# Hybrid decoder trunk on one core: the rows of the first two experts picked one expert at a time

## What is computed

```
x = x + mixed @ w_out[l]
x = x + hier_moe(rmsnorm(x, norm2_g[l]), router..., moe_w_gate[l], moe_w_up[l], moe_w_down[l])

# hier_moe: the best of 4 groups, the best 2 of its 8 experts; then for each expert, on its own tokens
hdn = jax.nn.silu(xb @ w_gate[e]) * (xb @ w_up[e])
y = hdn @ w_down[e]
# and out[token] += y * weight for the token's two experts
```

## Time and profile before

| | us |
|---|---|
| median of 3 runs | 1980.73 (1980.21 to 1994.71) |
| the profiled execution's own time | 1980.56 |
| its span, first to last instruction | 1978.7 |
| PE busy | 1656.9 (84%) |
| DVE busy | 609.6 (31%) |
| ACT busy | 277.4 (14%) |
| POOL busy | 163.5 (8%) |
| mean granted clock of TensorE | 0.959 of full |

### The profile page before, as it was taken

One profiled execution on the slowest core, in us unless ns is written; L12 is line 12 of the kernel. 1 busy time (PEld: TensorE's weight loads), 2 busy tenths in 40 slices (PEclk: granted clock), 3 DMA queues, 4 the chain that ended last, 5 costly groups with the idle time before them and its releaser, 6 DMA issues. The chain is left out here.

```text
span 1978.7 us, 23018 instructions
## 1 busy us (share of the span) xinstructions
PE 1656.9 (84%) x9408; PEld 979.9 (50%) x9408; DVE 609.6 (31%) x1296; ACT 277.4 (14%) x607; POOL 163.5 (8%) x185
## 2 busy tenths in 40 slices
PE   6999988897998768977489998898889877689772
PEld 3445656556554435544244465664565534345441
DVE  2263265713111123111224523565231111231113
ACT  2212233311000000000113123332100000000001
POOL 0010000002111010101100101000021101101001
PEclk9999999998999999999789999999989999999996
DMA  8312001056899998999651120103568999989995
GB/s 292 101 46 91 1 8 44 6 239 254 353 425 425 426 425 362 424 426 424 274 194 43 50 87 0 52 1 122 207 269 355 426 423 425 425 373 426 426 425 204
DMA packets 72615, 493.51 MB, mean 249 GB/s; under 512 B 24963, under 2 KB 26563, under 8 KB 36704
## 3 DMA queue, kind: packets, MB, share of 16 engines
q1 hardware_dynamic: 60160, 467.76, 57.7%
q0 software_dynamic: 12384, 24.80, 3.3%
HBM read 480.63 MB, written 28.11 MB: 257 GB/s over the span
## 5 line engine op out<-in xcount | busy, mean ns | idle before, releaser
L812 PE MATMUL banks<-RING,XS 128*64 128x256 f32 x3904 | 449.8, 386 | 84.0 <-DMA RING<-in_w_up 49.8
L812 PEld LDWEIGHTS banks<-RING,XS 128*64 128x64 f32 x3904 | 293.9, 139 | 258.4 <-DMA RING<-in_w_up 65.2
L827 PE MATMUL banks<-RING,XS 128*64 128x512 f32 x992 | 226.5, 597 | 39.9 <-DVE XS L1478 21.7
L536 PE MATMUL banks<-RING,XNT 128*128 128x512 f32 x512 | 224.0, 595 | 0.0
L1475 DVE SCALAR_TENSOR_TENSOR XS<-banks,TABLE,XS 128x256 f32<-128x256 f32 x60 | 29.0, 484 | 467.4 <-PE banks L812 467.4
L536 PEld LDWEIGHTS banks<-RING,XNT 128*128 128x128 f32 x512 | 96.6, 191 | 117.3 <-issue 116.8
L827 PEld LDWEIGHTS banks<-RING,XS 128*64 128x64 f32 x992 | 73.8, 136 | 149.8 <-issue 140.7
L1085 ACT ACTIVATE XS<-banks,TABLE 128x256 f32<-128x256 f32 x60 | 28.5, 474 | 827.3 <-PE banks L812 827.3
L1638 POOL DMA_INDIRECT y_rows<-XS,SOLVE x64 | 72.1, 1127 | 659.5 <-DVE XS L1500 659.5
L527 PE MATMUL banks<-XNT,RING 128*128 128x512 f32 x256 | 110.4, 593 | 1.8 <-DMA RING<-in_w_in_blocks 1.8
L1500 DVE COPY XS<-banks 128x512 f32<-128x512 f32 x64 | 44.3, 692 | 216.5 <-PE banks L827 216.5
(11 more groups left out here) (310 smaller groups left out, 1732.6 us busy)
## 6 DMA issues: line engine op xcount, KB each, us to landing
RING<-in_w_up SPq DMA_DIRECT2D x62, 2048.0 KB, 10.1
RING<-in_w_down SPq DMA_DIRECT2D x62, 2048.0 KB, 25.6
RING<-in_w_gate SPq DMA_DIRECT2D x60, 2048.0 KB, 26.5
RING<-in_w_in_blocks SPq DMA_DIRECT2D x12, 2048.0 KB, 8.3
RING<-in_w_out_blocks SPq DMA_DIRECT2D x4, 2048.0 KB, 7.8
TOK<-in_w_gate SPq DMA_DIRECT2D x4, 2048.0 KB, 26.1
y_rows<-TOK SPq DMA_DIRECT2D x4, 1024.0 KB, 25.1
SCAN<-in_w_gate SPq DMA_DIRECT2D x2, 2048.0 KB, 17.9
```

Of the source, the lines that this page charges most:

```text
L536: last = mm(bank[:, :], XNT[:, k, i * P:(i + 1) * P], w[:, k, :], start=(k == 0), stop=(k == KD - 1))
L812: last = mm(bank[f * CAP:(f + 1) * CAP, 0:256], rows[:, k, :], w[:, k, f * 256:(f + 1) * 256], start=(k == 0), stop=(k == KD - 1))
L827: last = mm(PS[5][n * CAP:(n + 1) * CAP, :], HT[:, j, f * CAP:(f + 1) * CAP], w[:, k, n * BN:(n + 1) * BN], start=(k == 0), stop=(k == KF ...
```

## The change

`pick_rows` takes one expert at a time: HOT's 64 columns of that expert are the stationary operand and X is the moving one, in two halves of 512 channels that lie on the two halves of the array, 8 products into bank 6. ACT copies the bank to `FIRST` (64 slots on each half of the partitions), `turn_picked` turns it by 16 products of 64x64 into bank 0 or 1, and DVE copies it with the scale into the expert's half of XT. Expert 1's picks stand behind expert 0's up products, its turning behind the turn of expert 0's hidden rows. DVE's copy for expert 0 stands ahead of the last steps on the slot numbers. And the eight loads of the combine count on two semaphores instead of four, so that the first two tiles wait for four loads together, and the last two for the next four. The diff, cut to its core:

```diff
+FIRST = view(XSb, 3328, BN)
...
-def pick_rows():
+def pick_rows(e):
+    for i in range(NT):
+        for n in range(2):
+            last = mm(PS[6][n * CAP:(n + 1) * CAP, :], HOT[:, i, e * CAP:(e + 1) * CAP], X3[:, i, n * BN:(n + 1) * BN],
+                      start=(i == 0), stop=(i == NT - 1))
+    last.then_inc(picked, 1)
+def turn_picked(e):
+    pe.wait_ge(pick_copied, e + 1)
+    halves = FIRST.rearrange("r (p k) -> r p k", k=KD)
     for k in range(KD):
-        for i in range(NT):
-            last = mm(PS[k // 4][:, (k % 4) * P:(k % 4 + 1) * P], X3[:, i, :].rearrange("t (p k) -> t p k", k=KD)[:, :, k],
-                      HOT[:, i, :], start=(i == 0), stop=(i == NT - 1))
-        if k % 4 == 3:
-            last.then_inc(picked, 1)
+        for n in range(2):
+            part = slice(n * CAP, (n + 1) * CAP)
+            last = mm(PS[e][part, k * CAP:(k + 1) * CAP], halves[part, :, k], ident[part, part], start=True, stop=True)
+    last.then_inc(picked, 1)
...
+    early = e if isinstance(e, int) else NE
+    if h == 0 or early == 1:
+        pe.wait_ge(xt_copied, i + 2 if early else 1)
     gate_or_up(of(0), PS[2], XT[:, :, h * CAP:(h + 1) * CAP]).then_inc(gate_ps, 1)
     gate_or_up(of(1), PS[3], XT[:, :, h * CAP:(h + 1) * CAP]).then_inc(up_ps, 1)
     if h == 1 and not last:
         pe.wait_ge(rows_full, 8 * (NE - 2) * layer + 16 * (i + 1))
         pe.sem_inc(pe_passed, 1)
         turn_rows(P, xt_ps)
+    if early == 0:
+        pick_rows(1)
     pe.wait_ge(hidden, e + 1)
     turn_hidden(ht_ps)
+    if early == 0:
+        turn_picked(1)
     pe.wait_ge(y2_copied, e + 1)
     pe.wait_ge(ht_copied, e + 1)
     down(of(2)).then_inc(y2_ps, 1)
 pe.wait_ge(first_hot, 1)
-pick_rows()
+pick_rows(0)
+turn_picked(0)
...
+def copy_picked(e):
+    act.wait_ge(picked, 2 * e + 1)
+    ac(FIRST, PS[6][:, :], ACT.Copy).then_inc(pick_copied, 1)
+copy_picked(0)
 def gates(first, last):
     for e in range(first, last):
         if e == 2:
             act.wait_ge(table_in, 32 * (layer + 1))
         act.wait_ge(gate_ps, e + 1)
         ac(HS, PS[2][:, 0:256], ACT.Silu, scale=BLK[:, e, 1:2] if e >= 2 else 1.0).then_inc(gated, 1)
+        if e == 0:
+            copy_picked(1)
...
 V.scalar_tensor_tensor(AT[:, :], SPOT, float(NBLK), rv(144, 8), ALU.mult, ALU.subtract).then_inc(routed, 1)
+def copy_picked(e):
+    dve.wait_ge(picked, 2 * e + 2)
+    V.tensor_tensor(XT[:, :, e * CAP:(e + 1) * CAP], PS[e][:, :].rearrange("p (k s) -> p k s", k=KD),
+                    G2K[:, :, None].to_broadcast([P, KD, CAP]), ALU.mult).then_inc(xt_copied, 1)
+copy_picked(0)
 spot_ij = SPOT.rearrange("p (j i) -> p i j", j=2)
 link(V.scalar_tensor_tensor(WTK.rearrange("p (i j) -> p i j", j=2), spot_ij, NE * CAP - 0.5, W2, ALU.is_lt, ALU.mult))
 link(V.tensor_scalar(SPOT, SPOT, -float(NE * CAP), None, ALU.add))
...
-def copy_rows(k0, k1, n):
-    k = k1 - k0
-    return V.tensor_tensor(XT[:, k0:k1, 0:n], PSALL[:, k0 * P:k1 * P].rearrange("p (k s) -> p k s", k=k)[:, :, 0:n],
-                           G2K[:, k0:k1, None].to_broadcast([P, k, n]), ALU.mult)
...
-dve.wait_ge(picked, 1)
-copy_rows(0, 4, P)
-dve.wait_ge(picked, 2)
-copy_rows(4, 8, P).then_inc(xt_copied, 1)
...
     hide(hidden, BLK[:, e, 1:2] if e >= 2 else None)
     dve.wait_ge(ht_ps, e + 1)
     copy_hidden(ht_copied)
+    if e == 0:
+        copy_picked(1)
     if h == 1 and e < NE - 1:
         dve.wait_ge(xt_ps, i + 1)
-        copy_rows(0, 8, P).then_inc(xt_copied, 1)
+        copy_rows().then_inc(xt_copied, 1)
...
-    dve.wait_ge(gathered[i], 32 * (layer + 1))
+    dve.wait_ge(gathered[i // 2], 64 * (layer + 1))
...
-    pool.dma_start(YG[n], yd[j * SEQ + i * P:j * SEQ + (i + 1) * P, :]).then_inc(gathered[i], 16)
+    pool.dma_start(YG[n], yd[j * SEQ + i * P:j * SEQ + (i + 1) * P, :]).then_inc(gathered[i // 2], 16)
```

More of the change, by code:

```diff
@@ L233, in build @@
             ctx.enter_context(nc.semaphore(n)) for n in ("scattered", "table_in", "rows_full"))
-        gathered = [ctx.enter_context(nc.semaphore(f"gathered{i}")) for i in range(NT)]
+        gathered = [ctx.enter_context(nc.semaphore(f"gathered{i}")) for i in range(2)]
         with nc.Block() as block:
@@ L314, in build @@
         combined = sem("combined")
-        first_hot, picked = sem("first_hot"), sem("picked")
+        first_hot, picked, pick_copied = sem("first_hot"), sem("picked"), sem("pick_copied")
         lam_rt, sgu_done = sem("lam_rt"), sem("sgu_done")
@@ L849, in expert @@
                         e = 2 * i + h
-                        if h == 0:
-                            pe.wait_ge(xt_copied, i + 1)
+                        early = e if isinstance(e, int) else NE
+                        if h == 0 or early == 1:
+                            pe.wait_ge(xt_copied, i + 2 if early else 1)
                         gate_or_up(of(0), PS[2], XT[:, :, h * CAP:(h + 1) * CAP]).then_inc(gate_ps, 1)
@@ L1452, in _, with copy_rows @@
                     V.scalar_tensor_tensor(AT[:, :], SPOT, float(NBLK), rv(144, 8), ALU.mult, ALU.subtract).then_inc(routed, 1)
+                    def copy_rows():
+                        return V.tensor_tensor(XT, PSALL[:, 0:2 * BN].rearrange("p (k s) -> p k s", k=KD), G2K[:, :, None].to_broadcast([P, KD, P]),
+                                               ALU.mult)
+                    def copy_picked(e):
[3 more added lines that the diff above has]
+                    copy_picked(0)
                     spot_ij = SPOT.rearrange("p (j i) -> p i j", j=2)
@@ L1455, in _ @@
                     link(V.tensor_scalar(SPOT, SPOT, -float(NE * CAP), None, ALU.add))
-                    cmp = XSb[:, 2048:2048 + NOV * NE].rearrange("p (b e) -> p b e", b=NOV)
+                    cmp = XSb[:, 2304:2304 + NOV * NE].rearrange("p (b e) -> p b e", b=NOV)
                     link(V.tensor_tensor(cmp, ends[:, None, :].to_broadcast([P, NOV, NE]),
```

## The result

The changed kernel takes **1998.8 us** (median of 20 runs, 1987.38 to 2017.25) beside 1986.26 us for the kernel before (median of 20 runs, 1980.21 to 1997.09). The ratio is 1.0072, 95% interval 1.0051 to 1.0092: about 14.3 us slower, between 10.1 and 18.3. Forecast were +2.5 us and a range that ended at +9.3. "Within 1%" was right, the size was not, and rival C (POOL's chain is late by more) is what happened.

A forecast was written before the change was run, and what follows sets the result against it. TensorE was taken to bound the kernel up to expert 3, weight transfers from there. Combine +5.1, picks -3.6 and POOL's chain +1.0 gave +2.5 on 1980.56 us: 1983.1, range 1977.5 to 1990.0.

The forecast's parts named there:

- rival C: Rows gathered by POOL reach PE later still: 1989.0 us at 7 late, 1995.8 at the bound of 10.4; chance 0.20.
- What bounds the kernel: Expert loops: TensorE sets the time up to expert 3, from there the weight transfers at some 425 GB/s.
- Only what is left of a gain at expert 3 counts: Start of the first loop: a lead at expert 0 counts only as far as it survives to expert 3.
- Expert 0's pick: First pick to expert 0's gates: 9.84 us in layer 0, 11.2 in layer 1; gates at 474.2 and 1452.0.
- Expert 1's pick: Expert 0's gates to expert 1's: 17.1 us instead of 12.25, leaving expert 1 1.6 and 2.0 us early.
- rival B: PE's clock stays low in expert 0's gates and turning after its new stops: +7.1, 1987.7 us; chance 0.20.
- together -3.6: Expert 1's gates: leads of 1.6 us in layer 0 and 2.0 in layer 1, summed over both layers.
- POOL's chain: Scatters, table read and gather meet the earlier loads; PE waits 0.5 us for rows per layer, +1.0 in all.
- The combine's semaphores: End of each layer: first addition waits for four loads, not two; 2.5 and 2.6 us lost, +5.1 in all.
- D: Start of the first loop: the first load's lead passes through, -13.4 + 5.1, 1972.3 us; chance 0.05.
- E: End of each layer: the combine's loads land close together, the merged wait costs nothing, 1978.0 us; chance 0.10.

The follow-up runs named there:

- The kernel after with four semaphores: The changed kernel with a semaphore for each tile of the combine, as before the change, early loads left as they are: 2001.01 us, ratio 1.0080.
- both repeats of before: The kernel before, unchanged, profiled a second and a third time: 1988.02 and 1982.06 us.
- its repeats: The changed kernel, with no further edit, profiled a second and a third time: 1999.38 and 2000.1 us.
- with the loads held: The changed kernel with the loop's first two weight loads held back until expert 0's down products are done: 1989.23 us, ratio 1.0003.

## Why the prediction was wrong, point by point

*What bounds the kernel* held: the mark behind the idle stretch decides, and what is lost or won there passes through, to within the 1.7 us of the overflow block. "Only what is left of a gain at expert 3 counts" is why 6 us at expert 0's gates came to nothing.

*Expert 0's pick* held in size. Forecast were 9.84 us to the gates in layer 0 and 11.2 in layer 1. Measured: 10.5, 9.0, 9.0 and 9.7, 10.3, 10.3. The spread is the moment at which the clock rises within the picks.

*Expert 1's pick* failed in layer 1. I had 17.1 us between the gates. Measured: 17.9, 17.6, 17.6 in layer 0; in layer 1 18.5 each time, where a part of expert 0's gates ran at the low clock (8.81 us for 7.13, rival B's mechanism, in one layer of two). The kernel after with four semaphores has 16.8 in both layers, so the chain itself was sized well; what adds 0.7 to 1.1 us in layer 0 of the others was not found. And the 2.0 us lead of layer 1 had been taken from a single profile, in which the gates of before ran slowly too: both repeats of before have them at full clock and expert 1's gates 28.6 us after the first pick, not 30.3. Against these, after's 28.8 in its repeats is no lead at all. Of "together -3.6" the repeats leave -2.0 in layer 0 (26.6 against 28.6) and +0.2 in layer 1; with the loads held, the marks show -0.2 and +0.3.

***POOL's chain* is the step that failed.** The prediction had the mechanism and sized it at "+1.0, both ends being equally near". PE waited 7.8, 7.6 and 7.2 us for rows, both layers together, in the three profiles of after, where I had 1.0. The mark moved by 4.0 and 4.4 us in after's own profile, and by 8.3 and 0.2 in each repeat, each against the 60.5 or, in the first profile, 62.2 of before. Three things were wrong in it:

- I let the loads meet the last scatter and the table, but not the gather: I had it land 8.3 us after its issue at most, or "several us earlier in the idle gap". But the gather, too, meets a load: the next gate matrix, issued as expert 0's down products end. Its rows were used 9.9 to 11.7 us after its issue where PE waited for them; the 8.3 was from the earlier trace rows.
- The delay of the gather's issue was sized too low. I had it 4 us late in layer 0 and 5.3 in layer 1; it was 5.0 and 5.9 in after's own profile, 7.6 and 5.4, then 7.2 and 5.2, in the repeats. It hangs on when the first load leaves. I took 3.7 us after the gates' start, ahead of the last scatter; in the three profiles of after it left 5.7 to 7.3 us after it, in layer 0 at a granted clock of 1.00, and what held it back was not found. Where it still went ahead of the last scatter (by 0.55 us in layer 0 of both repeats) POOL waited 6.26 and 5.62 us for that scatter instead of 0.80, and then 3.89 and 4.04 for the table. A faster PE made it worse, not better.
- The price of PE's stop was left out: behind the wait the turn takes up to 1.94 us instead of 1.16 and the down products up to 5.07 instead of 3.65; the granted clock of the stretch from 509 to 516 in after is 0.76.

The chance of 0.20 for C was too small for a term whose own bound was 10.4 us a layer, and the sum took the value next to its cheap end. Its bound of 1995.8 is 15 us above the run it was counted from; what was measured, +14.3, is there.

The Trainium skill's rule in DMA: Bandwidth & Descriptors, section "Queues, rings and completion order" (an engine takes turns between its queues, a packet at a time) would have let the small transfers through with no wait. The trace does not bear this out as a forecast of the time: POOL waits 6.6 us for a 24 KB table read with a 2 MB load ahead of it and 1.6 without.

*The combine's semaphores* held: 5.1 forecast; on the kernel before, 4.6 in the profile's two ends and +5.4 (0.4 to 10.1) in the time; and 23.1 against 20.6 us at each end in the repeats.

*Accounting.* With each kernel's three profiles averaged, the mark is 67.3 less 60.5 = 6.9 us later in layer 0, 62.7 less 61.1 = 1.6 in layer 1, the ends 4.8: 13.3 us. Between mark and last copy the three profiles of after take another 2.1 and 1.3 us on average, which makes 16.7, inside the measured 10.1 to 18.3. Of the 1.3 of layer 1, 0.7 arises at the overflow block, and the kernels with the old picks scatter as much (the stretch from mark to last copy is 441.8 to 443.7 us with them, 443.0 to 444.1 with the changed ones), so it is not shown to be a cost of the change. In layer 0 at least 1.1 of this stands in the last expert, whose down matrix lands later (PE waits 1.87 us for it instead of 0.78), in every kernel with the changed picks, the held ones included. What delays it was not found.

Of the rivals, B stands in part (layer 1's gates), and D and E are out: nothing of the first load's lead came through, and the merged wait is paid in full.

## What to carry to other kernels

When an edit makes an engine earlier, list what that engine's semaphores release, above all large loads, and lay them beside every small transfer of another queue that used to run in an idle stretch: here a small transfer issued behind a load paid up to 5.6 us (7.2 of waiting for the table instead of 1.6), about the length of that load (4.9 by 2,048 KB at 425 GB/s), and in a chain of three (scatter, read, gather) more than one of them paid. Then the repair is to hold the load, which cost nothing here, or to order the small chain first. And a lead that is read from one profile at one clock should not be counted until a second profile shows it: the 2.0 us of layer 1 were none.
